# Joining the value products of two steps in the first attention stage of a two-block transformer kernel

## What is computed

```python
# mixer_a, for each of 4 blocks of 128 latent queries; 16 heads of width 64
s_loc = einsum('bqhgd,bkhd->bhgqk', qs, ks) * scale     # own block and its neighbours
s_ctx = einsum('bqhgd,bkhd->bhgqk', qs, kc) * scale     # all 256 context keys
p = softmax(concatenate([s_loc, s_ctx, sink]))
o = einsum('bhgqk,bkhd->bqhgd', p_loc, vs) + einsum('bhgqk,bkhd->bqhgd', p_ctx, vc)
y = (o * silu(g)) @ w_o
# and the same for 2 blocks of context queries, on the context keys alone
```

## Time and profile before

| | us |
|---|---|
| median of three runs | 1157.46 |
| lowest and highest run | 1156.25, 1158.83 |
| the profiled execution | 1159.51 |
| its span, first to last instruction | 1157.7 |
| TensorE busy | 1103.7 (95%) |
| VectorE busy | 689.7 (60%) |
| ScalarE busy | 648.6 (56%) |
| GpSimd busy | 419.3 (36%) |

### The profile page before, as it was taken

How to read it: one execution, slowest core, us unless ns; L and a number is a source line. 1 busy time by engine, 2 the same in 40 slices (tenths; PEclk the granted TensorE clock), 3 DMA queues, 4 the chain that set the end, 5 groups by cost and what they waited for, 6 DMA issues and landing times.

```text
span 1157.7 us, 20083 instructions
## 1 busy us (share of the span) xinstructions
PE 1103.7 (95%) x7430; PEld 902.5 (78%) x7430; DVE 689.7 (60%) x1398; ACT 648.6 (56%) x1355; POOL 419.3 (36%) x513
## 2 busy tenths in 40 slices
PE   5999999999998899999999999999999999999996
PEld 2688778778885689877688887898878777888785
DVE  7474444454468625363787787745767775527745
ACT  5604555455556526643677777746567753457733
POOL 2633112212120334675400002416654326456781
PEclk9999999999999999999999999999999999999998
DMA  9641443533215621130201101052212404313112
GB/s 372 242 175 46 160 137 120 186 121 118 60 31 177 214 79 38 41 109 34 57 14 34 65 10 47 1 166 87 73 48 77 150 20 128 91 56 121 44 37 73
DMA packets 44524, 111.72 MB, mean 97 GB/s; under 512 B 14020, under 2 KB 16580, under 8 KB 44044
## 3 DMA queue, kind: packets, MB, share of 16 engines
q1 hardware_dynamic: 44428, 110.45, 28.8%
HBM read 103.75 MB, written 2.15 MB: 91 GB/s over the span
## 4 chain that ended last, share of the span: by engine, by line
PE 76%; DVE 11%; ACT 4%; issue 3%; DMA 3%; POOL 3%; SPq 0%; DVEq 0%; POOLq 0%; ACTq 0%
PE PS L699 31%; PE PS L682 15%; PE PS L819 8%; PE PS L807 7%; PE PS L1008 6%; PE PS L1076 3%; PE PS L734 2%; DMA AF<-wstream 1%; DVE AD L2433 1%; DMA sums<-AF 1%; PE PS L715 1%; DVE AF L2130 1%; POOL AR L2614 1%; DVE AR L2334 1%; PE PS L909 1%
## 5 line engine op out<-in xcount | busy, mean ns | idle before, releaser
L2614 POOL TENSOR_TENSOR AR<-AF,AR 128x256 fp32r<-128x256 f32 x396 | 304.0, 802 | 583.1 <-ACT AR L1177 583.1
L699 PE MATMUL PS<-AR 128*128 128x512 f32 (+1 forms) x2208 | 450.5, 360 | 3.0 <-POOL AR L2614 1.4
L699 PEld LDWEIGHTS PS<-AR 128*128 128x128 f32 x2208 | 364.0, 189 | 70.3 <-issue 10.5
L682 PE MATMUL PS<-AR 128*128 128x256 f32 (+4 forms) x1284 | 245.0, 327 | 5.0 <-DVE AF L1997 1.1
L682 PEld LDWEIGHTS PS<-AR 128*128 128x128 f32 (+1 forms) x1284 | 179.8, 190 | 40.6 <-issue 19.5
L1307 ACT ACTIVATE AF<-PS 128x512 f32<-128x512 f32 (+3 forms) x192 | 124.6, 649 | 108.4 <-PE PS L807 103.1
L1298 ACT ACTIVATE AF<-PS,AF 128x512 f32<-128x512 f32 (+3 forms) x192 | 140.8, 734 | 27.3 <-DVE AF L2410 18.1
L2069 DVE CUSTOM_DVE_ANT_0 PS<-PS,AF 128x512 f32<-128x512 f32 (+2 forms) x96 | 68.5, 714 | 130.1 <-PE PS L682 128.4
L807 PE MATMUL PS<-AF 128*128 128x128 f32 x864 | 127.4, 274 | 7.7 <-DVE AF L2020 4.5
L807 PEld LDWEIGHTS PS<-AF 128*128 128x128 f32 x864 | 100.0, 140 | 32.3 <-issue 16.9
L1177 ACT ACTIVATE AR<-AF 128x1024 fp32r<-128x1024 f32 x99 | 103.2, 1051 | 33.6 <-PE PS L1008 27.9
(11 more groups left out here) (220 smaller groups left out, 1138.3 us busy)
## 6 DMA issues: line engine op xcount, KB each, us to landing
AF<-wstream SPq DMA_DIRECT2D x171, 512.0 KB, 5.1
AR<-sums SPq DMA_DIRECT2D x12, 192.0 KB, 3.7
AF<-x_in SPq DMA_DIRECT2D x2, 1024.0 KB, 8.6
AD<-rows SPq DMA_DIRECT2D x4, 512.0 KB, 6.2
out<-AF SPq DMA_DIRECT2D x16, 128.0 KB, 1.9
AF<-AF SPq DMA_DIRECT2D x28, 64.0 KB, 2.0
AF<-rpb_band SPq DMA_DIRECT2D x8, 224.0 KB, 5.2
BIAS<-rpb_band SPq DMA_DIRECT2D x8, 224.0 KB, 4.4
```

Of the source, the lines that this page charges most:

```text
L682: mm = pe.matmul(out, stationary, moving, start=i == 0, stop=i == len(products) - 1)
L699: mm = pe.matmul(out[:, 0:t1 - t0], a, b, start=k == 0 and i == 0, stop=k == nk - 1 and i == 2)
L2614: ins = pool.tensor_tensor(w[:, 1, at:at + 256], raw(c)[:, at:at + 256], w[:, 0, at:at + 256].bitcast(F32), ALU.subtract)
```

## The change

In layer A the values are no longer made in each iteration between the first turn and the second scores. In iterations with an odd m they are made for two steps together, m-3 and m-2, after the first scores and before the first turn. Iterations with an even m make none. The last six steps (42 to 47) keep the old place and order. Nothing else is changed: the products, banks, buffers and waits are the same, and layers B and C keep their order.

```diff
+                def weighed_at(m):
+
+                    due = m - behind - 1
+                    if not m0 <= due < m1:
+                        return []
+                    if due >= m1 - 6:
+                        return [due]
+                    return [due - 1, due] if (due - m0) % 2 else []
+
...
                         banks_read(m == m0, 0, 1)
                         scores(2 * m)
+                    together = weighed_at(m) if values_first else []
                     if m0 <= m - behind < m1:
                         banks_read(m - behind == m0, 4, 5, 6)
+                    if len(together) == 2:
+                        for due in together:
+                            weigh_values(due)
+                    if m0 <= m - behind < m1:
                         turn(2 * (m - behind))
-                    ahead = values_first or m == m1
+                    ahead = len(together) == 1 if values_first else m == m1
                     if ahead and m0 <= m - behind - 1 < m1:
                         weigh_values(m - behind - 1)
...
-                    if not ahead and m0 <= m - behind - 1 < m1:
+                    if not ahead and not values_first and m0 <= m - behind - 1 < m1:
                         weigh_values(m - behind - 1)
```

## The result

The changed kernel is slower, and by more than forecast. All times are of one core in microseconds. The median before is now that of four runs; the forecast started from the 1157.46 of three.

A forecast was written before the change was run, and what follows sets the result against it. TensorE was taken to bound layer A's attention; copy waits, pair saving and corrections summed to 17.56 - 7.8 + 1.4 + 0.2 - 1.4 - 0.75 = +9.2 us, so 1157.46 became 1166.7 us, range 1160 to 1171.

The forecast's parts named there:

- TensorE bounds the stage: Layer A's attention, 109 to 322 us: TensorE busy 211.60 of 213 us, so each microsecond there counts in the run.
- The copy's wait: T2 waits for ScalarE's copy of T1's result once no values stand between: 2.76 us per six iterations, 17.56 over 2 to 39.
- The entry from scores into values: New transition on TensorE ahead of the joined values, not in the trace: taken as 0.09 us, between 0 and 0.175.
- The pair's saving: Joining two steps' values saves transitions and a fixed part: 0.41 us a pair, 7.8 us over nineteen pairs.
- The wait for the stream in iteration 17: Adaptive rows at L734 wait 1.7 us for a streamed chunk; 1.4 us of loss goes into this wait: minus 1.4.
- No other queue is passed ... Cost 0: The moved values issue only matmuls and pass no other engine's queue, VectorE's gate_output included: cost 0.
- copies that queue on ScalarE: Without a filler after T2 at m = 29 and 35, copies queue: 0.7 us twice, plus about 0.2 at iteration 22.
- From iteration 40 on: Iterations 40 to 43: T2 and VectorE's gate come earlier, shortening waits for VectorE: minus 0.75 us instead of a loss.
- Only the borders count: Rival: ScalarE's copy as good as hidden without the values, only the 7.8 us saving stands: 1149.7 us, chance 0.08.
- later waits swallow the loss: Rival: late transfers or VectorE near the end take up most of the loss, 0 to 2 us left: 1158.5, chance 0.06.
- The clock falls as well: Rival: many short TensorE waits lower the granted clock, adding some 11 us: 1178 us, chance 0.05.
- without that cover: If VectorE's work were not covered, each of some 15 groups would cost one VectorE operation, 0.68 us.

The follow-up runs named there:

- The experiment with the rows first: Changed kernel, but VectorE reads the modulation rows out of bank 7 ahead of the maximum of the first scores at s = 0: 1169.41 us, 1.0105 times before.
- the second trace: Trace of the changed kernel run again, unchanged: 1176.4 us, 1.0155 times the kernel before.
- the third chip: Changed kernel run a third time, unchanged, on another chip: 1171.6 us, 1.0121 times the kernel before.

## Why the prediction fell short

**What held.** That TensorE bounds the stage and every microsecond of waiting there is one of the run: 13.0 us more between 109 and 335 us, all of it idle time of TensorE. The copy's wait: T1 to T2 of 0.98, 1.38 and 1.60 us was forecast, and 0.94 to 1.00, 1.38 to 1.44 and 1.59 to 1.65 came. The entry from scores into values is 0.09 us, the value taken in the middle of 0 and 0.175. The Trainium skill's TensorEngine Tiling (Array Packing), section Tiling Modes, says that a change of mode drains the engine. That entering the 128*64 products costs time from either side agrees with it; the page gives no duration, and 0.09 and 0.175 are differences of slots, not the length of a drain. The pair's saving is 0.40, 0.37 and 0.39 us by position (for s = 2 and 3: 2.35 - 1.16 and 2.46 - 1.04 are taken out, 9.01 - 6.77 put in; the 0.40 of s = 0 and 1 is from iterations 30 and 36, where no row holds up the filler), against 0.41. The wait for the stream in iteration 17 is gone, as forecast, and more fully: L734 takes 1.84 us (215.97 to 217.81) instead of 3.53.

```profile
215.97 1.91 PE L734 MATMUL PS<-AF 128*12 128x512 f32 x16
217.81 0.74 PE L682 MATMUL PS<-AR 128*128 128x256 f32 x4
```

**The step that failed** is "No other queue is passed ... Cost 0". I followed the queues past which the values move, and they are passed by none. But the change also brings T2 forward, by 0.54 us at s = 0, and with it the filler behind T2. That filler opens bank 7 and needs VectorE's read of a modulation row (L1838), which stands in VectorE's queue behind a maximum of the new scores. Before, T2's lateness hid this. It costs 0.53 us more than before at iterations 6, 12, 18 and 24: 2.1 us. The experiment with the rows first took away 2.5 us, since the kernel before already waited some 0.1 us a place (its projection starts 0.25 us after T2, 137.11 to 137.36, that of the experiment 0.17).

**Terms that were mis-sized.** Between T1 of iterations 2 and 40 the shift grows by 14.2 us, where the terms for that stretch gave 17.56 - 7.8 + 1.6 - 1.4 = 10.0. The miss of 4.2 is made of
- bank 7: +2.1;
- late signals at s = 3, in no term: 0.49 + 0.57 + 0.83 = +1.9 in iterations 21, 33 and 39;
- small ones that repeat: T1 to T2 0.08 us above the forecast in a round of six, the saving 0.07 below, and T2 to the next T1 0.03 or 0.04 longer at each odd s, 0.10. A turn of 5 blocks behind values takes 0.53 us (120.03 to 120.56) and one behind a wait 0.49, where I took 0.46 throughout from a turn behind scores. That is 0.25 in a round, some +1.5;
- copies that queue on ScalarE: some +0.34 each near iterations 29 and 35 and nothing at 22, 0.7 us, where 0.7 twice and 0.2 were taken: -0.9;
- iteration 17: -1.69 instead of -1.4: -0.3.

These add up to 4.3. From iteration 40 on the shift falls by 0.66, where 0.75 was taken. This accounts for the 13.5 us of the stage. On the three chips on which it was timed the change cost 16.6, 17.3 and 14.0 us; the medians' 3 us above the stage's cost in the first pair are not traced to any place in the kernel, beyond the two profiled executions being where they are among their runs.

**The rivals.** "Only the borders count" falls with the 39 waits, "later waits swallow the loss" with the one such place that was already in the sum. "The clock falls as well" gave 1178, nearer to 1174.3 than the forecast, but is not what happened: the granted clock is 1.00 over the 226 us with the waits. The Trainium skill's TensorE: Matmul & The Clock Gate, section A second HAM failure mode: psum-queue depth-cycling, tells of another kernel in which frequent micro-idles made the clock swing; 39 waits of mostly 0.3 to 0.7 us did not do it here. The fall in iteration 9 of the second trace came behind 3.8 us of idle time.

**The range** was too narrow at the top. Its upper end allowed for every term being wrong, but for no wait that stood in no term. On the third chip the changed kernel took 1171.6 us, all but inside it; a hit there would have been luck, since the same terms were missing. Each new wait that shortens a distance makes all work behind it come earlier, and the cheapest allowance for that was in the text: one VectorE operation of 0.68 us a group, as "without that cover". I set it at nothing without looking for what was to be covered at T2's new time.

## What to carry to other kernels

Work between two uses of one buffer is cover for its evacuation: before moving it, read from the trace the shortest distance of the two uses without it, and set the saving against that. Then take every instruction that comes earlier by the move, not only the moved one, and ask for each bank or buffer it opens who has to release it, and what stands ahead of that in the releaser's queue. If the cover must go, a second buffer and the right order on the releasing engine come first; here the joining came to 0.2% only with both of them, in a kernel whose rows-first order was not run without the joining.

## What the hardware showed that I had not expected

Completion signals of TensorE can be late. Behind 52 products at L682 and 36 of joined values, the start of ScalarE's copy moved from 0.81 us after the turn's first product to 1.30 (iteration 21) and once to 4.18 (iteration 9 of the second trace), with neither DMA nor GpSimd at work in that time. It struck three of seven such iterations in each trace of the changed kernel, 33 and 39 always and a third that changed, and no first turn where the values stood alone; but one second turn was late by 1.2 us without a joined run. The ends of TensorE's products are modelled in the profile, so a late signal and late products can't be told apart by the rows of the turn alone; that the signals of turn and scores came 0.05 to 0.17 us apart in the places shown, where their work is 0.58 apart, speaks for the signal. The cause stays open.

It also means that two traces of the changed kernel differ by some 6 us over the stage (12.9 and 18.8), so that a difference between two single traces of it carries that much doubt, and the medians decide.
